# A hybrid decoder layer in f32 on one core: attention values in pairs, other queues at both ends, and another order of output parts

## The chip, the core and the metric

The kernel runs on one of the eight cores of a Trainium2 chip. The metric is device time in microseconds. Kernel and change are each one program with one launch.

## The reference

One step of a one-layer trunk, for a prompt of 2048 tokens and for 8 sequences of 4 new tokens each ("sample", 32 rows). Model width 1024, everything in f32. Cut to what matters:

```
u = rmsnorm(x, g_mix);  z = u @ w_in + b_in            # 1024 -> 1792
q (8 x 64) | k (2 x 64) | v (2 x 64) | xb (512) | yb (512) = split(z)
attn = softmax(q k^T / 8 - slope * distance, window 128, with a sink per head) @ v
xc   = causal conv of width 4 over xb
r, ig = sigmoid(block_diag(xc, w_a)), sigmoid(block_diag(xc, w_i))
a = exp(-8 r softplus(-lam));  h_t = a_t h_{t-1} + sqrt(1 - a_t^2) (ig_t xc_t)
mix = concat(attn, h * gelu(yb))                       # 512 + 512
h1 = x + mix @ w_out + b_out
y  = h1 + (silu(gate) * up) @ w_ffn_out,  gate, up = rmsnorm(h1) @ w_ffn_in    # hidden 2816
y  = rmsnorm(y, g_final)
```

The outputs are y for prompt and sample, and the last keys, values, conv rows and states of both.

## The kernel before, in words

**Tiling.** Activations lie transposed: features on the 128 partitions, tokens along the free dimension. The prompt goes through in four blocks (b = 0 to 3) of 512 tokens. The 32 sample rows ride along with block 0 up to the input projection and with block 3 from the output projection on; there a unit is 544 columns wide and is computed in two halves of 272 (`chunks`, `wide_at`), elsewhere in one piece of 512. A *unit* is a strip of 128 output features: K, V, four Q, eight of the recurrent branch (x and y, `UH` on), eight of the output projection (`U_O`), then those of the FFN. A unit is a sum over 8 tiles of 128 input features (kt). f32 precision comes from three products per tile with operands split in a high and a low part: x_hi w_hi (L724), x_lo w_hi (L725), x_hi w_lo (L726).

**Banks.** PSUM has eight banks: three (`G`, bank0 to bank2) go round for the units, two (`S`, bank3 and bank4) hold scores, two (`TB`) transposes, one (`V`, bank7) the attention values. `bank_of` and `place_of` give a half its bank; `gemm` makes PE wait until the half that used the bank last has been read.

**Order.** Each engine's program is written out by hand and they meet in semaphores. On PE, `mixers` has eight steps s, one per unit of the recurrent branch: `scores(s)` (L859; queries of 128 tokens, four heads), `attend(s - 2)` (L891; probabilities times values), a part of the unit's tiles, in odd steps `gates(s // 2)` (L901), then `probs_T(s - 1)` (L873, transposes of probabilities that POOL has normalised), then the rest of the unit. The scores products take quarters of the array and attend's take half of its columns; the unit products take all of it. ACT and DVE copy the transposed probabilities to SBUF (`pT`, L1313 and L1725); attend waits for these copies. `gates` uses bank7 and a G bank for the first channel group, the S banks for the others.

After step 7 come the *parts* of the output projection: its last four tiles (4 to 7) are the recurrent results, whose last one (`lmix_ready`, DVE L1784) is late, and tiles 0 to 3 the attention (`amix_ready`, L1789). So three units (in the last block three halves) are begun together: first tiles 4 and 5, then 6, then the four attention tiles of each, last tile 7 of each.

**Weights.** SP loads each unit's raw weights into one of two buffers; ACT makes the high part (`split`, L1179) and DVE the low part (L1572) in a ring of three slots. A slot is free when the unit that used it is done. In block 0 the parts of 22 units are also stored to HBM and loaded again in later blocks.

**Start and end.** At the start SP asks for four rows of tiles x_tok, ACT for the identity matrix, the sample rows xs_tok and the vectors. PE transposes x_tok (L1102) and xs_tok (L1126), ACT and DVE sum squares and copy, PE spreads 1/rms along the rows (`along`, L757), and then per tile DVE scales (L1607), ACT makes x_hi (L1228), DVE x_lo (L1613) and PE multiplies for units K and V (`first_units`). At the end four tiles of y_p and one of y_s go out: SP asks in the order y_p 0, 1, 2, y_s in four pieces, y_p 3.

Of the kernel before, what the change touches and what calls it, by code (L numbers as in the profile page):

```python
# [33 lines left out]
P = 128  # L34
# [57 lines left out]
def hymba_layer(nc, x_p, x_s, cache_k, cache_v, conv_in, h_in, units, vecs, w_a, w_i, sinks_p, sinks_s,  # L92
# [3 lines left out]
    DB, DT = x_s.shape[0], x_s.shape[1]  # L96
# [52 lines left out]

    def place_of(b, u, c):  # L150


        j = JOB[b, u, c]
        return j - (j > 3)
# [5 lines left out]
    with ctx:  # L160
# [156 lines left out]
        def bank_of(b, u, c):  # L317
            return S[0] if JOB[b, u, c] == 3 else G[place_of(b, u, c) % 3]
# [211 lines left out]
        def _(sp):  # L530
# [40 lines left out]

            for m in range(QB):
                sp.dma_start(x_tok[:, m, :], x_p[0, m * P:(m + 1) * P, :]).then_inc(row_in[m], 16)
            for u in range(NU):
                load_raw(0, u)
                if RAW <= u < KEEP + RAW:
                    store_parts(u - RAW)
# [7 lines left out]
            for n, m in enumerate(END):  # L585
                sp.wait_ge(end_act, n + 1)
                sp.wait_ge(end_dve, n + 1)
                if m < QB:
                    y_out[m % 2].by(sp.dma_start(y_p[0, bass.ds((NB - 1) * T + m * P, P), :], x_tok[:, m, :]))
                else:  # L590
                    for t in range(DT):
                        sp.dma_start(y_s[:, t, :], y_tok[t * DB:(t + 1) * DB, 0, :]).then_inc(ys_out, 16)
# [3 lines left out]
        def _(pool):  # L596
# [80 lines left out]
            for done_, n in ((cache_out, 2), (kv_out, N_KV_OUT), (state_out, N_STATE_OUT), (ys_out, DT)):  # L677
                pool.wait_ge(done_, 16 * n)
# [5 lines left out]
        def _(pe):  # L684
# [10 lines left out]
            def gemm(b, wide, u, hi, lo, tile_ready=None, kts=None, only=None, begins=0):  # L695
# [11 lines left out]
                for c, (c0, c1) in enumerate(chunks(wide)):  # L707
                    if only is not None and c != only:
                        continue

                    j = JOB[b, u, c]
                    if first and j > 3:
                        pb, pu, pc = JOBS[j - 4 if j < 7 else j - 3]
                        if wide_at(pb, pu) and pc == 0:
                            pe.wait_ge(read_in_half if pu < UO0 else freed_half, pu + 1 if pu < UO0 else pu - UO0 + 1)
                        else:
                            units_read(pe, pb, pu + 1)
                    out = bank_of(b, u, c)[:, 0:c1 - c0]
                    for kt in kts:
                        if tile_ready and (c == 0 or only == c):  # L720
                            tile_ready(kt)
                        h = w_h[:, kt * P:(kt + 1) * P]
                        l = w_l[:, kt * P:(kt + 1) * P]
                        nc.tensor.matmul(out, h, hi[:, kt, c0:c1], start=(first and kt == kts[0]), stop=False)  # L724
                        nc.tensor.matmul(out, h, lo[:, kt, c0:c1], start=False, stop=False)  # L725
                        mm = nc.tensor.matmul(out, l, hi[:, kt, c0:c1], start=False, stop=(kt == kt_of[u] - 1))  # L726
                    if wide and c == 0 and final:
                        mm.then_inc(gemm_half, 1)
# [110 lines left out]
            def mixers(b, last):  # L839
# [65 lines left out]
                for s in range(NUN):  # L905
                    scores(s)
                    if s >= 2:
                        attend(s - 2)
                    wide = wide_at(b, UH + s)
                    if wide:  # L910
                        gemm(b, wide, UH + s, x_hi, x_lo, None, None, 0)
                    else:
                        cut = KT // 2 if s % 2 == 0 else KT - 3 if s == 1 else KT - 2
                        gemm(b, wide, UH + s, x_hi, x_lo, None, list(range(cut)))
# [24 lines left out]
                ahead = [(0, 0), (0, 1), (1, 0)] if last else [(0, 0), (1, 0), (2, 0)]  # L939
# [8 lines left out]
                attend(NUN - 1)  # L948
                for m, c in ahead:
                    part(m, recurrent[2:3], c)  # L950
                for m, c in ahead:
                    part(m, list(range(KT - LC)), c)
                for m, c in ahead:
                    part(m, recurrent[3:], c)
                if last:
                    part(1, None, 1)
# [161 lines left out]

            pe.wait_ge(ident_here, 16)
            for m in range(QB):  # L1120
# [15 lines left out]
            alongx_done.by(along(rstd_x, True))  # L1136
            first_units()
# [14 lines left out]
        def _(act):  # L1152
# [13 lines left out]
            act.dma_start(ident[:, :], ident_in).then_inc(ident_here, 16)  # L1166
            act.dma_start(xs_tok[:, :], x_s.rearrange("b t d -> t b d")).then_inc(xs_in, 16)
# [334 lines left out]
            split(0, 0)  # L1502
# [5 lines left out]
            for kt in FIRST_ACT[:2]:  # L1508
                first_moved(kt)
            x_keep(0, True)  # L1510
            first_moved(FIRST_ACT[2])
# [21 lines left out]
            for n, m in enumerate(END):  # L1533
# [4 lines left out]
                else:  # L1538
                    act.wait_ge(state_out, 16 * N_STATE_OUT)
                    act.wait_ge(smp_pe, 9)  # L1540
                    A(y_tok[0:NS, 0, 0:512], o[0:NS, :], ACT.Copy, scale=rstd_t[0:NS, m:m + 1]).then_inc(end_act, 1)


        @block.vector
        def _(dve):
# [474 lines left out]
            for kt in FIRST_DVE[:2]:  # L2020
                first_moved(kt)
            reciprocals(0, True, std_x, rstd_x, stdx_ready, rstdx_ready)
            first_moved(FIRST_DVE[2])
# [159 lines left out]
```

## Time and profile before

| | us |
|---|---|
| median of 3 runs | 2217.58 |
| lowest, highest | 2216.32, 2218.53 |
| profiled execution | 2216.64 |
| its span in the trace | 2214.5 |
| PE busy in it | 2182.7 (99%) |
| DVE busy | 1155.6 (52%) |
| ACT busy | 835.4 (38%) |
| mean granted clock of PE | 0.997 |

Times in the trace count from the start of the span. An engine's busy time is the time in which at least one of its instructions runs; matmuls overlap, so the pace is read from one start to the next. What stands in brackets behind a row is the idle time just before it and what ended it. The granted clock has two levels, 1.2 and 2.4 GHz; 1.00 is the higher.

### The profile page before, as it was taken

Reading aid. Unit: us, or ns where it says so; the run is one execution under the profiler, and the core shown is the slowest. Engines: PE = TensorE matmul, PEld = TensorE weight load, DVE = VectorE, ACT = ScalarE, POOL = GpSimd, SP = SyncE. Lnnn points to the kernel's source line nnn. Section 1 sums busy time; section 2 is a strip of 40 time slices with the busy share of each in tenths; the row PEclk is TensorE's granted clock in tenths of the full one; section 3 lists DMA queues with packets and bytes.
Section 4 is the critical chain, followed back from the end, with each engine's and each line's share of the span. In section 5 each row is a group of like instructions: output and inputs, shape, how many; then the busy total and the mean of one; then the engine's idle time right before and its main releaser. Section 6 shows DMA issues by size and latency. Waiting matters only on the chain.

```text
span 2214.5 us, 29659 instructions
## 1 busy us (share of the span) xinstructions
PE 2182.7 (99%) x12131; PEld 1839.8 (83%) x12131; DVE 1155.6 (52%) x1981; ACT 835.4 (38%) x1372; POOL 155.6 (7%) x186
## 2 busy tenths in 40 slices
PE   7999999999999999999999999999999999999997
PEld 7878888888877888888877888888887799999997
DVE  5777535445376544434448654444537654444443
ACT  5773323242374322224258322223336532222223
POOL 1330000000041000000013000000003200000000
PEclk9999999999999999999999999999999999999999
DMA  7455224222634222232453432222244332222221
GB/s 272 155 186 187 90 89 153 96 86 86 214 129 171 95 95 95 90 100 83 138 180 113 171 100 94 93 95 96 87 179 153 117 105 87 86 86 86 88 88 66
DMA packets 78923, 264.81 MB, mean 120 GB/s; under 512 B 9521, under 2 KB 13825, under 8 KB 78772
## 3 DMA queue, kind: packets, MB, share of 16 engines
q1 hardware_dynamic: 73504, 246.58, 32.3%
q0 software_dynamic: 3232, 9.80, 1.3%
q10 hardware_dynamic: 2052, 6.53, 0.7%
q8 instruction: 97, 1.59, 0.3%
q14 instruction: 38, 0.31, 0.0%
HBM read 231.04 MB, written 32.84 MB: 119 GB/s over the span
## 4 chain that ended last, share of the span: by engine, by line
PE 92%; DVE 3%; ACT 2%; issue 1%; POOL 1%; DMA 0%; ACTq 0%; DVEq 0%; POOLq 0%
PE bank L724 29%; PE bank L726 29%; PE bank L725 29%; PE bank L891 1%; PE bank L873 1%; POOL s_p L611 1%; PE bank L859 1%; PE bank L901 1%; DVE s_p L1706 1%; PE bank L821 0%; PE bank L773 0%; DMA xs_tok<-in_x_sample 0%; ACT s_p L1306 0%; DVE xc L1742 0%; DVE xc L1737 0%
## 5 line engine op out<-in xcount | busy, mean ns | idle before, releaser
L724 PE MATMUL bank<-x_hi,w_hi 128*128 128x512 f32 (+1 forms) x2224 | 787.2, 354 | 3.3 <-DVE x_lo L1613 3.2
L726 PE MATMUL bank<-x_hi,w_lo 128*128 128x512 f32 (+1 forms) x2224 | 780.3, 351 | 0.0
L725 PE MATMUL bank<-x_lo,w_hi 128*128 128x512 f32 (+1 forms) x2224 | 779.0, 350 | 0.0
L1179 ACT ACTIVATE w_hi<-w_raw 128x1024 fp32r<-128x1024 f32 (+1 forms) x294 | 304.6, 1036 | 1006.1 <-PE bank L726 973.7
L724 PEld LDWEIGHTS bank<-x_hi,w_hi 128*128 128x128 f32 x2224 | 418.9, 188 | 70.6 <-issue 11.0
L725 PEld LDWEIGHTS bank<-x_lo,w_hi 128*128 128x128 f32 x2224 | 419.2, 188 | 56.7 <-issue 1.7
L726 PEld LDWEIGHTS bank<-x_hi,w_lo 128*128 128x128 f32 x2224 | 418.7, 188 | 56.4
L1572 DVE TENSOR_TENSOR w_lo<-w_raw,w_hi 128x1024 fp32r<-128x1024 f32 (+1 forms) x294 | 351.4, 1195 | 123.7 <-ACT w_hi L1179 123.7
L724 PE MATMUL bank<-a_hi,w_hi 128*128 128x512 f32 (+1 forms) x1168 | 412.0, 353 | 2.8 <-DVE a_lo L1784 1.5
L726 PE MATMUL bank<-a_hi,w_lo 128*128 128x512 f32 (+1 forms) x1168 | 411.5, 352 | 0.0
L725 PE MATMUL bank<-a_lo,w_hi 128*128 128x512 f32 (+1 forms) x1168 | 410.9, 352 | 0.0
L724 PEld LDWEIGHTS bank<-a_hi,w_hi 128*128 128x128 f32 x1168 | 219.4, 188 | 38.1 <-issue 5.4
L725 PEld LDWEIGHTS bank<-a_lo,w_hi 128*128 128x128 f32 x1168 | 219.5, 188 | 30.9
L726 PEld LDWEIGHTS bank<-a_hi,w_lo 128*128 128x128 f32 x1168 | 219.3, 188 | 30.7
L611 POOL TENSOR_SCALAR s_p<-s_p,rec 128x256 f32<-128x256 f32 x128 | 127.2, 1009 | 1360.3 <-DVE rec L1720 1360.3
L1999 DVE TENSOR_TENSOR hT<-bank,hT 128x512 f32<-128x512 f32 (+1 forms) x120 | 70.8, 592 | 243.8 <-PE bank L726 243.4
L1586 DVE TENSOR_TENSOR a<-bank,rinv 128x512 f32<-128x512 f32 (+1 forms) x110 | 65.1, 592 | 215.6 <-PE bank L726 213.6
L1586 DVE TENSOR_TENSOR gt<-bank,rinv 128x512 f32<-128x512 f32 (+1 forms) x110 | 64.9, 591 | 203.0 <-PE bank L726 202.5
L1306 ACT ACTIVATE s_p<-s_p,nm 128x256 f32<-128x256 f32 x128 | 63.2, 495 | 32.2 <-DVE sd L1712 31.8
L1466 ACT ACTIVATE a_hi<-a 128x512 fp32r<-128x512 f32 (+1 forms) x88 | 56.3, 639 | 35.8 <-DVE a L1984 33.8
L1980 DVE SCALAR_TENSOR_TENSOR gt<-th,gt 128x512 f32<-128x512 f32 (+1 forms) x88 | 61.1, 694 | 5.0 <-ACT th L1463 5.0
L1984 DVE SCALAR_TENSOR_TENSOR a<-gt,a 128x512 f32<-128x512 f32 (+1 forms) x88 | 61.7, 701 | 3.0
(306 smaller groups left out, 1580.5 us busy)
## 6 DMA issues: line engine op xcount, KB each, us to landing
w_raw<-in_units SPq DMA_DIRECT2D x222, 512.0 KB, 3.2
w_raw<-in_units SPq DMA_DIRECT2D x64, 448.0 KB, 3.1
w_hi<-keep SPq DMA_DIRECT2D x51, 512.0 KB, 3.3
w_lo<-keep SPq DMA_DIRECT2D x51, 512.0 KB, 4.5
w_kept<-keep SPq DMA_DIRECT2D x30, 512.0 KB, 4.4
keep<-w_hi SPq DMA_DIRECT2D x22, 512.0 KB, 5.3
keep<-w_lo SPq DMA_DIRECT2D x22, 512.0 KB, 6.4
x_tok<-in_x_prompt POOLq DMA_DIRECT2D x12, 512.0 KB, 5.3
```

The costliest lines, as they stand in the source:

```text
L611: ins = nc.gpsimd.tensor_scalar(s_p[:, s % 2, hh, :], s_p[:, s % 2, hh, :], rec[:, qb % 2, head:head + 1], None, ALU.mult)
L724: nc.tensor.matmul(out, h, hi[:, kt, c0:c1], start=(first and kt == kts[0]), stop=False)
L725: nc.tensor.matmul(out, h, lo[:, kt, c0:c1], start=False, stop=False)
L726: mm = nc.tensor.matmul(out, l, hi[:, kt, c0:c1], start=False, stop=(kt == kt_of[u] - 1))
L1179: A(w_hi[:, slot(b, u), 0:n], w_raw[:, u % RAW, 0:n], ACT.Copy).then_inc(w_hi_ready, 1)
L1306: A(s_p[:, s % 2, hh, :], s_p[:, s % 2, hh, :], ACT.Exp, bias=nm[:, s % 2, hh:hh + 1], accum_out=rs[:, s % 2, hh:hh + 1])
L1466: act_hi.by(A(a_hi[:, f, 0:w], a32[:, n % 2, 0:w], ACT.Copy))
L1572: TT(w_lo[:, slot(b, u), 0:n], w_raw[:, u % RAW, 0:n], w_hi[:, slot(b, u), 0:n], ALU.subtract).then_inc(w_ready, 1)
L1586: return lambda src, c0, c1: TT(dst(c0, c1), src, rinv[:, c0:c1], ALU.mult)
L1980: link(STT(out=gt[:, 0:w], in0=th[:, 0:w], scalar=1.0, in1=gt[:, 0:w], op0=ALU.add, op1=ALU.mult))
L1984: act_f.by(STT(out=a32[:, n % 2, 0:w], in0=gt[:, 0:w], scalar=0.5, in1=a32[:, n % 2, 0:w], op0=ALU.mult, op1=ALU.mult))
L1999: evacuate(b, last, u, lambda src, c0, c1: TT(hT[:, m, c0:c1], src, hT[:, m, c0:c1], ALU.add))
```

## The change

Six edits.

1. In `mixers`, attend(s - 3) and attend(s - 2) both stand behind scores(s) in the odd steps from 3 on, and none in even steps. In even steps of narrow blocks one more of the unit's tiles (5 of 8) comes ahead of `probs_T`. Since attend(0) also held PE back until gates(0) had been read, step 2 of block 0 now waits for that by itself.
2. In the last block a fourth half, (1, 1), is begun with the other three. Its bank is S[0], and it leaves the turns of the G banks (`TURNS`).
3. In block 0 the parts are in another order: unit 0 ends after the first two attention tiles of unit 2.
4. The identity and xs_tok are asked for on SP's queue, ahead of x_tok and behind its second tile.
5. y_s goes out as one request on ACT's queue, after all copies of the end.
6. PE multiplies the identity by itself, 8 times ahead of the first transposes and 20 times after `along`; nobody reads the results. At the start ACT's first split stands behind its first copy, and copies stand behind `x_keep` (ACT) and behind the reciprocals (DVE).

```diff
+    J_LAST = JOB[NB - 1, U_O[1], 1]
+    TURNS = [j for j in range(len(JOBS)) if j not in (3, J_LAST)]
+    TURN = {j: i for i, j in enumerate(TURNS)}
     def place_of(b, u, c):
-        j = JOB[b, u, c]
-        return j - (j > 3)
+        return TURN[JOB[b, u, c]]
...
-            return S[0] if JOB[b, u, c] == 3 else G[place_of(b, u, c) % 3]
+            return S[0] if JOB[b, u, c] in (3, J_LAST) else G[place_of(b, u, c) % 3]
...
+            sp.dma_start(ident[:, :], ident_in).then_inc(ident_here, 16)
             for m in range(QB):
                 sp.dma_start(x_tok[:, m, :], x_p[0, m * P:(m + 1) * P, :]).then_inc(row_in[m], 16)
+                if m == 1:
+                    sp.dma_start(xs_tok[:, :], x_s.rearrange("b t d -> t b d")).then_inc(xs_in, 16)
...
-                else:
-                    for t in range(DT):
-                        sp.dma_start(y_s[:, t, :], y_tok[t * DB:(t + 1) * DB, 0, :]).then_inc(ys_out, 16)
...
-                    if first and j > 3:
-                        pb, pu, pc = JOBS[j - 4 if j < 7 else j - 3]
+                    if first and j == J_LAST:
+                        sc_read.wait(pe, b, NUN)
+                        gates_read.wait(pe, b, LC)
+                    elif first and j > 3:
+                        pb, pu, pc = JOBS[TURNS[TURN[j] - 3]]
...
                     scores(s)
-                    if s >= 2:
+                    if s >= 3 and s % 2 == 1:
+                        attend(s - 3)
                         attend(s - 2)
+                    if s == 2 and wide:
+                        gates_read.wait(pe, b, 1)
...
-                        cut = KT // 2 if s % 2 == 0 else KT - 3 if s == 1 else KT - 2
+                        cut = KT // 2 + 1 if s % 2 == 0 else KT - 3 if s == 1 else KT - 2
...
-                ahead = [(0, 0), (0, 1), (1, 0)] if last else [(0, 0), (1, 0), (2, 0)]
+                ahead = [(0, 0), (0, 1), (1, 0), (1, 1)] if last else [(0, 0), (1, 0), (2, 0)]
...
                 attend(NUN - 1)
+                for m, c in ahead[3:]:
+                    part(m, recurrent[:2], c)
                 for m, c in ahead:
                     part(m, recurrent[2:3], c)
...
+                if b == 0:
+                    part(0, list(range(KT - LC)))
+                    part(1, list(range(KT - LC)))
+                    part(2, list(range(2)))
+                    part(0, recurrent[3:])
+                    part(2, list(range(2, KT - LC)))
+                    part(1, recurrent[3:])
+                    part(2, recurrent[3:])
...
-                if last:
-                    part(1, None, 1)
...
+            def idle_products(bank, n):
+                for _ in range(n):
+                    nc.tensor.matmul(bank[:, 0:P], ident[:, :], ident[:, :], start=True, stop=True)
+
             pe.wait_ge(ident_here, 16)
+            idle_products(V, 8)
...
             alongx_done.by(along(rstd_x, True))
+            pe.wait_ge(moved_dve, 2)
+            idle_products(G[0], 20)
             first_units()
...
-            act.dma_start(ident[:, :], ident_in).then_inc(ident_here, 16)
-            act.dma_start(xs_tok[:, :], x_s.rearrange("b t d -> t b d")).then_inc(xs_in, 16)
...
-            split(0, 0)
...
-            for kt in FIRST_ACT[:2]:
-                first_moved(kt)
+            first_moved(FIRST_ACT[0])
+            split(0, 0)
             x_keep(0, True)
+            first_moved(FIRST_ACT[1])
...
+            act.wait_ge(end_act, len(END))
+            act.wait_ge(end_dve, len(END))
+            act.dma_start(y_s.rearrange("b t d -> t b d"), y_tok[0:NS, 0, :]).then_inc(ys_out, 16)
```

PE at the start of the program, before:

```order
L1102 MATMUL bank<-ident,x_tok 128x128 x14
L1126 MATMUL bank<-ident,xs_tok 128x32 x8
L1102 MATMUL bank<-ident,x_tok 128x128 x18
L757 MATMUL bank<-ident,rstd_x 128x128 x4
L760 MATMUL bank<-ident,rstd_x 128x32
L724 MATMUL bank<-x_hi,w_hi 128x272
```

and of the change (L1146 is the idle product, L1125 the transposes):

```order
L1146 MATMUL bank<-ident 128x128 x8
L1125 MATMUL bank<-ident,x_tok 128x128 x14
L1156 MATMUL bank<-ident,xs_tok 128x32 x8
L1125 MATMUL bank<-ident,x_tok 128x128 x18
L766 MATMUL bank<-ident,rstd_x 128x128 x4
L769 MATMUL bank<-ident,rstd_x 128x32
L1146 MATMUL bank<-ident 128x128 x20
L733 MATMUL bank<-x_hi,w_hi 128x272
```

Two groups of idle products have come in; the rest keeps its order.

PE in block 1, steps 4 and 5 of the mixer, before (L859 scores, L891 attend, L901 gates, L873 transposed probabilities; "..." stands for unit products):

```order
L859 MATMUL bank<-kT,qT 64x192 x8
L891 MATMUL bank<-pT,v_tok 64x256 x4
...
L873 MATMUL bank<-ident,s_p 128x128 x8
...
L859 MATMUL bank<-kT,qT 64x192 x8
L891 MATMUL bank<-pT,v_tok 64x256 x4
...
L901 MATMUL bank<-xc,gates_w 128x512 x2
L873 MATMUL bank<-ident,s_p 128x128 x8
```

and of the change (L868, L900, L910, L882):

```order
L868 MATMUL bank<-kT,qT 64x192 x8
...
L882 MATMUL bank<-ident,s_p 128x128 x8
...
L868 MATMUL bank<-kT,qT 64x192 x8
L900 MATMUL bank<-pT,v_tok 64x256 x8
...
L910 MATMUL bank<-xc,gates_w 128x512 x2
L882 MATMUL bank<-ident,s_p 128x128 x8
```

The attend of the even step has moved behind that of the odd step, eight instructions in a row.

PE in the last block behind the last attend, before (bank0, bank1, bank2 are the halves (0, 0), (0, 1), (1, 0)):

```order
L891 MATMUL bank7<-pT_102,v_tok_63 64x256 x4
L724 MATMUL bank0<-a_hi_55,w_hi_51 128x272
L725 MATMUL bank0<-a_lo_56,w_hi_51 128x272
L726 MATMUL bank0<-a_hi_55,w_lo_52 128x272
L724 MATMUL bank1<-a_hi_55,w_hi_51 128x272
L725 MATMUL bank1<-a_lo_56,w_hi_51 128x272
```

and of the change (bank3 is the half (1, 1)):

```order
L900 MATMUL bank7<-pT_102,v_tok_63 64x256 x4
L733 MATMUL bank3<-a_hi_55,w_hi_51 128x272
L734 MATMUL bank3<-a_lo_56,w_hi_51 128x272
L735 MATMUL bank3<-a_hi_55,w_lo_52 128x272
L733 MATMUL bank3<-a_hi_55,w_hi_51 128x272
L734 MATMUL bank3<-a_lo_56,w_hi_51 128x272
```

The half that came last as a whole before now runs beside the other three, tile by tile.

## Rows read from the trace of the kernel before

**Rows 1.** Page, part 1: busy us, share of the span, instructions.
```profile
PE 2182.7 (99%) x12131; PEld 1839.8 (83%) x12131; DVE 1155.6 (52%) x1981; ACT 835.4 (38%) x1372; POOL 155.6 (7%) x186
```

**Rows 2.** PE's waits: instruction, released by, us in total, times, longest.
```profile
PE bank L891 <- ACT pT L1313: 2.6, 4, 0.8
...
PE bank L873 <- POOL s_p L611: 0.9, 2, 0.5
PE bank L859 <- ACT ii L1321: 0.6, 2, 0.3
...
PE bank L724 <- DVE a_lo L1789: 0.2, 1, 0.2
```

**Rows 3.** Timeline of the start: start us, us, engine, instruction, idle before.
```profile
2.21 0.39 ACTq L1166 DMA_DIRECT2D ident<-in_ident_in  x1
...
9.44 3.17 PE L1102 MATMUL bank<-ident,x_tok 128*128 128x128 f32 x14 [9.44 <-DMA ident<-in_ident_in]
9.50 1.23 DVE L2011 CUSTOM_DVE_ANT_0 hT<-x_tok 128x1024 f32<-128x1024 f32 x1 [0.36 <-DMA x_tok<-in_x_prompt]
...
11.99 1.06 ACT L1501 ACTIVATE y_tok<-xs_tok 32x1024 f32<-32x1024 f32 x1 [3.85 <-DMA xs_tok<-in_x_sample]
...
13.15 2.18 PE L1102 MATMUL bank<-ident,x_tok 128*128 128x128 f32 x18
...
15.85 1.13 PE L757 MATMUL bank<-ident,rstd_x 128*128 128x128 f32 x8 [0.51 <-ACT xT L1493]
...
20.48 0.60 PE L724 MATMUL bank<-x_hi,w_hi 128*128 128x272 f32 x1 [3.17 <-DVE x_lo L1613]
```

**Rows 4.** Busy by stretch (us, busy): PE, PEld, DVE, ACT, POOL, PEclk, DMA share, GB/s.
```profile
20.00:30.00 10.00, 9.52 (x55) 9.42 (x56) 9.78 (x15) 5.09 (x9) 0.00 (x0) 0.70 0.88 332
...
45.00:60.00 15.00, 14.97 (x120) 14.73 (x118) 2.45 (x2) 4.70 (x8) 0.00 (x0) 1.00 0.91 321
...
98.60:118.60 20.00, 19.68 (x166) 16.65 (x168) 19.14 (x50) 17.98 (x40) 9.01 (x9) 1.00 0.45 159
```

**Rows 5.** Timeline of DVE, the last two x_lo of the start.
```profile
29.74 1.53 DVE L1613 TENSOR_TENSOR x_lo<-a,x_hi 128x544 fp32r<-128x544 f32 x2
```

**Rows 6.** Timeline of PE in block 1, steps 1 and 3.
```profile
612.15 0.88 PE L859 MATMUL bank<-kT,qT 64*64 64x192 f32 x16
...
613.29 0.40 PE L725 MATMUL bank<-x_lo,w_hi 128*128 128x512 f32 x1
...
630.67 0.88 PE L859 MATMUL bank<-kT,qT 64*64 64x192 f32 x16
631.48 1.08 PE L891 MATMUL bank<-pT,v_tok 128*64 128x256 f32 x8
...
632.83 0.39 PE L725 MATMUL bank<-x_lo,w_kept 128*128 128x512 f32 x1
```

**Rows 7.** DVE's waits in block 0, 98.6 to 130 us.
```profile
DVE pT L1725 <- PE bank L873: 0.4, 2, 0.2
```

**Rows 8.** Timeline of POOL and of PE in block 1, step 2.
```profile
621.68 3.63 POOL L611 TENSOR_SCALAR s_p<-s_p,rec 128x256 f32<-128x256 f32 x4 [2.48 <-DVE rec L1720]
...
626.92 1.04 PE L873 MATMUL bank<-ident,s_p 128*128 128x128 f32 x8
```

**Rows 9.** Timeline of ACT and PE, output units of block 0.
```profile
156.70 1.06 ACT L1179 ACTIVATE w_hi<-w_raw 128x1024 fp32r<-128x1024 f32 x1 [4.45 <-PE bank L726]
...
159.08 0.50 PE L724 MATMUL bank<-a_hi,w_hi 128*128 128x512 f32 x1 [1.06 <-DVE w_lo L1572]
```

**Rows 10.** Timeline of PE, output parts of the last block.
```profile
1753.45 0.36 PE L724 MATMUL bank<-a_hi,w_hi 128*128 128x272 f32 x1 [1.55 <-DVE a_lo L1784]
```

**Rows 11.** Timeline of SP at the end.
```profile
2204.39 2.86 SPq L592 DMA_DIRECT2D out_y_s<-y_tok  x4
2207.36 0.37 SPq L589 DMA_DIRECT2D out_y_p<-x_tok  x1
```

**Rows 12.** What the core's DMA moved, 40 slices of 2195 to 2214 us.
```profile
GB/s 0 0 0 0 0 0 0 0 0 0 0 0 0 34 0 0 0 250 397 423 388 405 405 414 414 276 86 181 379 405 267 0 0 0 0 0 0 0 0 0
```

More of the change, by code:

```diff
@@ L676, in _ @@
             pool.dma_start(nh_p[0], outr_p[CONV_W - 1:CONV_W, :]).then_inc(state_out, 16)
-            for done_, n in ((cache_out, 2), (kv_out, N_KV_OUT), (state_out, N_STATE_OUT), (ys_out, DT)):
+            for done_, n in ((cache_out, 2), (kv_out, N_KV_OUT), (state_out, N_STATE_OUT), (ys_out, 1)):
                 pool.wait_ge(done_, 16 * n)
@@ L948, in mixers @@
                 attend(NUN - 1)
+                for m, c in ahead[3:]:
+                    part(m, recurrent[:2], c)
                 for m, c in ahead:
                     part(m, recurrent[2:3], c)
[L951 to L954, printed above, removed]
-                if last:
-                    part(1, None, 1)
+                if b == 0:
[6 more added lines that the diff above has]
+                    part(2, recurrent[3:])
+                else:
+                    for m, c in ahead:
+                        part(m, list(range(KT - LC)), c)
+                    for m, c in ahead:
+                        part(m, recurrent[3:], c)
                 for u in U_O[2 if last else 3:]:
@@ L2019, in _ @@
             first_sum(3)
-            for kt in FIRST_DVE[:2]:
-                first_moved(kt)
+            first_moved(FIRST_DVE[0])
             reciprocals(0, True, std_x, rstd_x, stdx_ready, rstdx_ready)
+            first_moved(FIRST_DVE[1])
             first_moved(FIRST_DVE[2])
```

## The prediction

> **What bounds the kernel now.** I read the page first. TensorE (PE) is busy for 2182.7 of 2214.5 us [rows 1], so the weight products are the floor and only the time in which PE waits, runs at the lower clock or changes mode can be won. The list of PE's waits came second: ahead of its four passes through the mixer it waits 2.6 us for copies of transposed probabilities, and under 1 us each for POOL and for gate values [rows 2]. Third, the timeline of the start: the first weight product stands at 20.48 us [rows 3]. Fourth, the busy table by stretch: the granted clock is 0.70 in 20 to 30 us, and 1.00 later at 120 products in 15 us, 0.125 us each [rows 4]. Then the stretches in which the change acts: a mixer [rows 6], the output parts [rows 9, 10] and the stores at the end [rows 11, 12].
>
> The sum is made against the profiled execution, 2216.64 us (its span 2214.5 us), which lies 0.94 us under the median of 2217.58.
>
> **Start.** The identity is asked for at 2.21 us on ACT's queue, behind nothing of its own, but on the chip's transfers beside 2 MB of x_tok, and PE starts with it at 9.44; xs_tok holds ACT until 11.99, and split, copies, square root and PE's four row products at 15.85 follow in series [rows 3]. Now SP asks for the identity first and for xs_tok between rows 1 and 2. The last row of x_tok lands at 9.50 today [rows 3]; 192 KB now stand ahead of it on its queue, at 332 GB/s [rows 4] 0.6 us at most, since part of them crossed its way before too; I take 10.0. From there: DVE's square sum 1.2 us, two square roots and one copy on ACT 1.1, so PE's row products begin near 12.35 instead of 15.85: 3.5 us. Behind them ACT has one more copy ahead of x_hi, DVE its split; I charge 0.1 us. The first product could start at 17.1.
>
> The idle products are new. Four such f32 products of 128 columns with their loads fill 8 records in 1.13 us at the higher clock [rows 3], 0.26 us each; 20 of them take 5.1 us, from 13.7 to 18.9. They end 1.8 us after the first x_lo is there, so they delay the first product, but at 18.9 PE comes straight from work and should be at the higher clock. Today it comes from 3.2 us of waiting and runs its first products at about half pace; the last of the 96 products of the first two units starts near 34.7. With 96 x 0.126 = 12.1 us from 18.9 it ends near 31.0. DVE does not stop this: its last two x_lo end at 31.27 today [rows 5], 27.9 after a shift of 3.4, plus two tiles of products (3.0) is 30.9. That gives about 3.9 us. Bounds: 5 (clock and rows better) and 0 (next paragraph). The first 8 idle products lie in time in which PE waits for rows 0 and 1, and row 3 is what counts; cost nothing, and if row 3 came 2 us sooner they would still be hidden.
>
> What the clock does decides. The first 14 transposes took 3.17 us, 0.23 each, and the 18 at 13.15 took 2.18, 0.12 each [rows 3]: the clock rose while PE did little but transposes. I go by that. The Trainium skill (TensorE: Matmul & The Clock Gate, Part 4: PE-mode transpose) says transposes do not count as activity that brings the full clock; the two rows speak against it. By it the row products and idle products would run at the lower level, and that is the first rival.
>
> A second rule speaks against moving requests between queues: the Trainium skill (DMA: Bandwidth & Descriptors, Issuing engines are not separate DMA queues) says that it saves only issue time, because all queues interleave on the same engines. By it the identity would have come early already. The trace shows 64 KB asked for at 2.21 and not used before 9.44 [rows 3], so here the queue matters. If the rule held, transposes would still run from 9.44 to 15.33 and the row products begin 0.5 us earlier than now, not 3.5.
>
> **Values in pairs.** In each of four blocks three pairs of attends stand behind one scores instead of behind two. Scores alone, to the second product behind them, take 613.29 - 612.15 = 1.14 us; scores and attend 632.83 - 630.67 = 2.16 [rows 6]. So an attend costs 1.02 us. Its 8 records take 1.08 with the last one 0.38 long, so they follow each other by 0.10: 0.80 of pure work [rows 6]. A second attend directly behind the first should cost 0.80: 0.2 us a pair, 0.6 us a block. Bounds 0 and 0.22. Besides, attend(0) moves from step 2 to step 3, and its wait for the copy (2.6 us over four blocks, 0.6 to 0.8 each) [rows 2] goes. Blocks 1 to 3: 3 x (0.6 + 0.6) = 3.6 us.
>
> What is late next? In even steps probs_T comes sooner. In block 1 POOL ends at 621.68 + 3.63 = 625.31 and PE transposes at 626.92 [rows 8]; without wait and attend (0.61 + 1.02) and with the one tile more ahead of it (3 x 0.23) it comes at 625.98: 0.67 us to spare. The copies that attend(s-3) reads are a step older than before. Scores of odd steps start earlier by 1 us, far behind the softmax that frees their banks.
>
> Block 0 is another matter. Its steps work on 544 columns and DVE also splits weights: in 98.6 to 118.6 DVE is busy 19.14 of 20 us [rows 4]. There PE's waits for gate values (0.6) and probabilities [rows 2] come from DVE's chain, and a faster PE only waits longer. DVE itself waits 0.4 us for PE's transposes in this stretch and its successor [rows 7] and some 0.3 in the one ahead, and those come earlier now. I take 0.7 us for block 0; bounds 0 and 2.3.
>
> **Order of block 0's parts.** Unit 3 of the output waits 1.06 us for w_lo [rows 9], whose ring slot is freed by the end of unit 0: ACT's split at 156.70, first product at 159.08, 2.6 us from the end of unit 0 near 156.5. Today two parts of three products (6 x 0.231 = 1.4 us) lie between; afterwards two tiles of attention and two last parts, 12 x 0.231 = 2.77. The wait goes: 1.1 us, plus a switch of 0.1 once; I take 1.2, bounds 0.9 and 1.2. The last recurrent tile, now wanted earlier, was ready 1.4 us before that place.
>
> **Fourth half sum.** In the last block PE waits 1.55 us for the last a_lo [rows 10], 0.2 for the attention one [rows 2], and 0.4 of the 0.9 us for probabilities [rows 2]. The half (1, 1) in the scores' bank puts 7 tiles x 3 x 0.126 = 2.6 us of existing work ahead of that wait. Both a_lo waits go: 1.7. The 0.4 goes if DVE's chain gets ahead by the shorter step 6, as it should (DVE waited there for PE's unit). 2.1 us, bounds 1.5 and 2.1. No product is added.
>
> **End.** SP asks four times for y_s, 2204.39 to 2207.25, and only then for the last y_p, 2207.36 [rows 11]; its data was ready at 2204.98. ACT now asks once for y_s. The issue comes 2.3 us sooner, but 2.2 MB must drain: from 2203.1 at some 410 GB/s it ends near 2208.5 instead of 2209.7 [rows 12]. I take 1.2 us, bounds 0.9 and 2.3.
>
> **Sum.** 3.9 + 3.6 + 0.7 + 1.2 + 2.1 + 1.2 = 12.7 us; 2216.64 - 12.7 = 2203.9, on the scale of the median 2204.9.
>
> **Rivals.** (a) The start brings nothing, because the requests land no sooner (part of this chance) or the clock is low: the 20 idle products take twice 5.1, end near 23 to 24 or rise midway; the start brings 0 and the sum 8.8: 2208.8. For it: a break of a microsecond ahead of them. Against: the 18 transposes at 0.12. (b) Switching between attends costs as before and block 0 gives nothing: 2.4 + 0.7 less, with the copies' wait still gone: 2208.0. For it: nobody has put two attends side by side in this trace. (c) What PE wins is waited for later at the weights: everything won ahead of the last block (3.9 + 0.7 + 1.2 + 2.4) is lost: 2213.1. Against: each unit's loads are released by PE's own progress, and DMA is 36% busy. (d) Slower: the even steps. With attend gone from ahead of probs_T only the 0.67 us remain; if POOL's 3.6 to 4.8 us norm comes later than that by t in each of 12 even steps, PE pays 12 t, and above t = 1.06 us all is lost; at t = 1.5 it is 2223. For it: POOL's row ends that near. Against: DVE, which releases POOL, is itself ahead when PE's even unit ends sooner. That a term simply isn't there is (a) to (c).
>
> **Numbers.** Forecast 0.63, (a) 0.14, (b) 0.11, (c) 0.08, (d) 0.04. 0.2% of the median is 4.4 us, about what can be told from no change: 2213.1. Forecast, (a), (b) fall under it, (c) lies on it: faster 0.88, same 0.08, slower 0.04. The range reaches from the upper bounds (2204.9 less 4: 1.1 at the start, 1.6 in block 0, 1.1 at the end) to beyond (a): 2200.5 to 2209.5.
>
> **What would show it.** First weight product at 18 to 19.5 us and granted clock near 1.00 in 20 to 30; PE's waits for pT, for w_lo at output unit 3 and for the last a_lo gone; two attends in 1.9 us; span from the last matmul to the end shorter by 1.2. Wrong if the first product is behind 20 us, or if waits for s_p or gates above 1 us stand in even steps of blocks 1 to 3.

## The result, and the profile after

The changed kernel takes 2205.05 us (median of 5 runs, 2204.99 to 2205.6), the kernel before 2217.58 (5 runs, 2216.32 to 2218.53): a ratio of 0.9945 with a 95% interval of 0.9933 to 0.9956, 12.5 us less. The forecast was 2204.9. The profiled execution took 2204.99 us, its span is 2203.1. Two executions at a low mean granted clock (0.632 in one of the kernel before, 0.85 in one of e10) took 3185.77 and 2370.93 us and are in no ratio below.

The page of after, part 1 (answers to [rows 1]): PE's busy time is 2.4 us longer, though the span is 11.4 shorter.

```profile
PE 2185.1 (99%) x12187; PEld 1845.8 (84%) x12187; DVE 1153.5 (52%) x1981; ACT 835.0 (38%) x1372; POOL 156.6 (7%) x186
```

All waits of PE in after (us in total, times, longest) answer to [rows 2]. The waits for pT, w_lo and a_lo are gone; of 0.9 us for s_p 0.4 is left, in block 0.

```profile
PE bank L1146 <- DMA ident<-in_ident_in: 2.6, 1, 2.6
PE bank L766 <- ACT xT L1523: 0.9, 1, 0.9
PE bank L868 <- ACT ii L1351: 0.7, 2, 0.5
PE bank L1125 <- DMA x_tok<-in_x_prompt: 0.6, 2, 0.4
PE bank L745 <- ACT sq L1276: 0.6, 1, 0.6
PE bank L882 <- POOL s_p L617: 0.4, 1, 0.4
PE bank L868 <- issue: 0.3, 1, 0.3
PE bank L733 <- ACT ii L1351: 0.2, 1, 0.2
```

The start of after, on the timeline (start us, us, engine, instruction, idle before), answers to [rows 3]:

```profile
0.73 0.39 SPq L578 DMA_DIRECT2D ident<-in_ident_in  x1
...
2.62 3.78 PE L1146 MATMUL bank<-ident 128*128 128x128 f32 x16 [2.62 <-DMA ident<-in_ident_in]
...
6.20 2.34 PE L1125 MATMUL bank<-ident,x_tok 128*128 128x128 f32 x14
...
10.94 1.23 DVE L2045 CUSTOM_DVE_ANT_0 hT<-x_tok 128x1024 f32<-128x1024 f32 x1
...
13.26 1.13 PE L766 MATMUL bank<-ident,rstd_x 128*128 128x128 f32 x8 [0.89 <-ACT xT L1523]
...
14.65 4.73 PE L1146 MATMUL bank<-ident 128*128 128x128 f32 x40
...
17.11 0.72 DVE L1647 TENSOR_TENSOR x_lo<-th,x_hi 128x544 fp32r<-128x544 f32 x1
...
19.14 0.37 PE L733 MATMUL bank<-x_hi,w_hi 128*128 128x272 f32 x1
```

To find where the rest of the time went I took the same instructions in both traces and compared their start times. These are the ones of after:

```profile
56.66 0.88 PE L868 MATMUL bank<-kT,qT 64*64 64x192 f32 x16 [0.28 <-issue]
...
139.62 1.08 PE L900 MATMUL bank<-pT,v_tok 128*64 128x256 f32 x8
...
599.64 0.88 PE L868 MATMUL bank<-kT,qT 64*64 64x192 f32 x16
...
677.34 1.08 PE L900 MATMUL bank<-pT,v_tok 128*64 128x256 f32 x8
...
1734.87 1.08 PE L900 MATMUL bank<-pT,v_tok 128*64 128x256 f32 x8
...
2187.55 1.05 PE L745 MATMUL bank<-ones,sq 128*128 128x1 f32 x8 [0.56 <-ACT sq L1276]
2190.71 1.04 PE L801 MATMUL bank<-ident,yg 128*128 128x128 f32 x8
```

| from ... to | before, us | after, us | gained | forecast |
|---|---|---|---|---|
| start of the span ... scores(0) of block 0 | 60.25 | 56.66 | 3.59 | 3.9 |
| ... last attend of block 0 | 83.99 | 82.96 | 1.03 | 0.7 |
| ... scores(0) of block 1 | 461.33 | 460.02 | 1.31 | 1.2 |
| mixers of blocks 1, 2 (each) | 78.82, 78.81 | 77.70, 77.70 | 1.12, 1.11 | 1.2, 1.2 |
| mixer of block 3 | 77.76 | 76.16 | 1.60 | 1.2 + 0.4 |
| last attend of block 3 ... row sums of y | 455.11 | 452.68 | 2.43 | 1.7 |
| row sums ... last transposes | 3.16 | 3.16 | 0 | 0 |
| last transposes ... end of the span | 11.67 | 12.39 | -0.72 | +1.2 |

The stretches between the blocks' mixers and the next scores differ by 0.04 us at most: what is won stays won. The sum is the span's 11.4 us. The execution profiled before lay 0.94 us under its median, the one after 0.06 under, so the medians differ by about 1 us more than the profiles.

### The profile page after: what moved, and what is told of

Its sections match the earlier page's. It is cut to its first block, busy times and chain, and to the rows that moved or that the text cites. A ratio compares the mean times of both kernels' runs of the same rounds, so it can differ in the third digit from the quotient of the medians.

```text
span 2203.1 us, 29774 instructions
## 1 busy us (share of the span) xinstructions
PE 2185.1 (99%) x12187; PEld 1845.8 (84%) x12187; DVE 1153.5 (52%) x1981; ACT 835.0 (38%) x1372; POOL 156.6 (7%) x186
## 3 DMA queue, kind: packets, MB, share of 16 engines
q8 instruction: 97, 1.59, 0.3%
## 4 chain that ended last, share of the span: by engine, by line
PE 95%; DVE 2%; ACT 1%; issue 1%; POOL 0%; DMA 0%; SPq 0%; DVEq 0%; ACTq 0%; POOLq 0%
PE bank L733 30%; PE bank L735 30%; PE bank L734 30%; PE bank L900 1%; PE bank L882 1%; PE bank L910 1%; PE bank L868 1%; PE bank L830 0%; PE bank L782 0%; POOL s_p L617 0%; DMA x_tok<-in_x_prompt 0%; DVE s_p L1740 0%; ACT s_p L1336 0%; PE bank L1146 0%; DVE xc L1776 0%
```

## The experiments

The start varies from run to run. In the four profiles with the old requests (before, e4, e6, e7) DVE's sum of row 3 began at 9.50, 9.41, 10.64 and 10.43 us, but the scores of block 0 came at 60.25, 61.25, 60.03 and 61.20: there it is not the rows that set the start. PE's last 18 transposes took 2.18, 4.10, 2.55 and 3.89 us, and the two in which they kept half pace are the two late ones. In after, e1, e2 and e11 the scores (56.66, 57.30, 57.42, 57.18) follow row 3 by 45.7 to 45.8 us each time. The two means lie 3.5 us apart, so the 3.59 of the table is a fair value. So the verdicts rest on stretches between two instructions of one profile, and the medians only confirm them.

### The parts of the mixers and the last block, alone (e4, e6, e7)

Each is one edit made on the kernel before. Pairs:

```diff
-                    if s >= 2:
+                    if s >= 3 and s % 2 == 1:
+                        attend(s - 3)
                         attend(s - 2)
-                        cut = KT // 2 if s % 2 == 0 else ...
+                        cut = KT // 2 + 1 if s % 2 == 0 else ...
```

> The kernel before with the values in pairs alone (attend(s-3) and attend(s-2) behind scores(s) of odd steps; one more tile ahead of the probabilities' transposes in even steps). Theory 1 (the mixers' gain of 1.0 to 1.2 a block comes from the pairs alone): 4.3 to 4.8 us faster than before, 2212.8 to 2213.3, the waits for pT gone. Theory 2 (part of what the mixers gained was handed on by the earlier start or by the order of block 0's parts): blocks 1 to 3 still gain 1.1 each, block 0 less than 0.5: 3.3 to 3.8 us faster, 2213.8 to 2214.3.

Measured 2212.77 us (10 runs), ratio 0.9977 (0.9968 to 0.9987) to a before of 2218.14. Mixers: block 0 82.99 instead of 83.99, block 1 77.71, block 2 77.69, block 3 76.17: 1.00, 1.11, 1.12 and 1.59 us, the same as in after to 0.03 us. 4.8 us come from the pairs alone. The last block stayed at 455.11.

The order of block 0's parts (the diff is that of the change, the branch for b == 0):

> The kernel before with only the new order of block 0's output parts. Theory 1 (the gain of 1.3 us is the wait of unit 3 for w_lo and one switch, whatever else is changed): from the last attend of block 0 to the first scores of block 1 it takes 460.0 us instead of 461.33, the wait for w_lo is gone; the time falls by 1.3 us. Theory 2 (the wait only moves: to the next unit's w_lo, or back as soon as PE reaches the part at the old time): 461.1 to 461.4 us, no gain.

460.01 us instead of 461.33, and the wait for w_lo is no longer in the list: 1.32 us. Median 2215.92 (11 runs) against 2217.88, ratio 0.9992 (0.9983 to 1.0001), in which one such term is hardly seen. Theory 1.

The fourth half sum, with TURNS and the bank of the scores as in the change:

> The kernel before with only the fourth half sum in a bank of the scores in the last block (and the tables of turns that it needs). From the last attend of the last block to the first row sums of y it takes 455.11 us in before and 452.68 in after, 2.43 less, where I had 1.7. Theory 1 (the two waits for a_lo and what PE loses when it restarts behind them and in the half's own start, all in this edit): 2.3 to 2.5 less, and block 3's mixer stays at 77.76: the time 2.3 us under before. Theory 2 (0.7 of it comes from the pairs, which leave PE later relative to DVE): 1.6 to 1.8 less.

452.68 us instead of 455.11, 2.43 less, and the mixer of block 3 as before, 77.77; median 2215.51 (11 runs), ratio 0.9992 (0.9983 to 1.0001). Theory 1. The 0.7 us above the two waits can be read in before's timeline: between two products of 0.126 us stand three breaks. The first product behind the last a_lo starts 1.83 us behind the one ahead, though the wait is 1.55 [rows 10], and the next follows by 0.20 and not 0.126. The break at the attention a_lo takes 0.46 + 0.20, its wait 0.17; the separate start of (1, 1) behind the wait 0.28 + 0.20. Less the usual pace that is 1.77 + 0.40 + 0.22 = 2.4 us. So these waits cost their own length and some 0.22 us for the restart.

### The end (e1, e2)

```diff
-            act.dma_start(y_s.rearrange("b t d -> t b d"), y_tok[0:NS, 0, :])   # ACT
+                else:                                                           # SP, ahead of the last y_p
+                    for t in range(DT):
+                        sp.dma_start(y_s[:, t, :], y_tok[t * DB:(t + 1) * DB, 0, :]).then_inc(ys_out, 16)
```

> The kernel after, with the sample outputs y_s stored as before: four requests of 8 rows on SP, ahead of the last y_p. Theory 1 (the tail is the one request of ACT, whose last 1.3 us run at about 100 GB/s after everything else has drained): the four requests hold the last y_p back to about 2195.3, but end at full rate, so the stores end near 2197.0 to 2197.6 instead of 2198.2: the time falls by 0.6 to 1.2 us, to 2203.9 to 2204.5. Theory 2 (my forecast's: the four issues of 2.9 us ahead of the last y_p are what the end waits for): the time rises by 1.2 us, to 2206.2.

e2 has the one request in that place on SP.

> The kernel after, with y_s stored in one request (the same one, 32 rows) by SP ahead of the last y_p, not by ACT behind everything. Theory 1 (late start of the one request at about 100 GB/s): it starts 0.7 us sooner, beside the y_p stores, and the last y_p is asked for at about 2193.6, before the first three have drained: the stores end near 2197, the time is 1.0 to 1.6 us under after, 2203.5 to 2204.1. Theory 2 (the request's own shape sets the end wherever it stands): no more than 0.3 us from after.

Last transposes to the end of the span: e1 11.72 us, e2 12.40, after 12.39, before 11.67. Medians 2204.84 and 2205.39; e1's 0.21 us under after is less than theory 1 said, since in its profiled execution the rows came 0.7 us later at the start (scores at 57.30). Theory 1 is right for e1 in the stretch and wrong for e2: moving the request gains nothing, its form keeps the tail. What the core's DMA moved in 40 slices of 2187 to 2204 us (0.425 us each), in after:

```profile
GB/s 0 0 0 0 0 0 0 0 0 116 414 386 405 414 395 405 395 414 395 405 366 366 106 87 116 58 0 0 0 0 0 0 0 0 0 0 0 0 0 0
```

and in e1:

```profile
GB/s 0 0 0 0 0 0 0 0 0 0 0 279 405 395 434 395 386 395 434 405 241 96 145 386 386 405 58 0 0 0 0 0 0 0 0 0 0 0 0 0
```

In after the 128 KB of y_s move at about 100 GB/s as a tail of four slices, and in e2, where they are asked for ahead of the last y_p, they are again the tail (125, 87, 116, 77, 19). In e1 (and before, [rows 12]) there is a hole of three slices ahead of the last y_p instead. By these times SP's issues set its length: the last y_p is asked for at 2195.89 in e1 and begins to move some 0.8 us later, as the first does behind its request at 2190.99. At what rate y_s could move in that hole can't be told from it. The change filled the hole and grew the tail. On ACT's queue 36 packets are counted in after for the 32 rows; the four requests take 64 (640 less 576), the four y_p requests 576 for 512 rows. So beyond the rows it is 16 packets for a request of y_p, 8 for one of 8 rows and 4 for the single one, which has 4 outer groups. That fits a request on 4 of the 16 engines at a quarter of the 400 GB/s, but no view here shows the engines one by one.

### The idle products (e3, e11)

```diff
-            idle_products(G[0], 20)
```

> The kernel after without the 20 idle products ahead of the first weight product (the first 8 stay). Theory 1 (they buy the full clock): the first weight product is at 17.8 us instead of 19.1, but the granted clock in 20 to 30 us falls back to about 0.7, and PE is 1 to 3 us behind at the scores of block 0: time 2206 to 2208. Theory 2 (the clock is up anyway from the transposes, row products and the shorter break of 3 us): the first units are bound by DVE's copies; the scores come 0 to 1.2 us sooner, time 2203.9 to 2205.

Median 2205.69, ratio 0.9945 (0.9933 to 0.9958) to 2218.14. The first weight product moves to 17.52 us, but from DVE's sum of row 3 to the scores it takes 46.28 us (10.53 to 56.81) instead of 45.72. So the 20 are worth 0.56 us, less than theory 1 said (1 to 3), and the gain of theory 2 isn't there. Busy by stretch, PE alone (us, busy, PEclk, DMA share, GB/s), in e3:

```profile
14.00:16.00 2.00, 0.31 (x2) 0.72 0.50 141
16.00:18.00 2.00, 0.48 (x2) 0.50 0.90 209
18.00:20.00 2.00, 2.00 (x10) 0.50 1.00 248
20.00:22.00 2.00, 2.00 (x12) 0.57 1.02 399
```

and in after:

```profile
14.00:16.00 2.00, 2.00 (x18) 1.00 0.42 107
16.00:18.00 2.00, 2.00 (x21) 1.00 0.73 191
18.00:20.00 2.00, 2.00 (x20) 1.00 0.92 250
```

In e3 the granted clock goes to 0.50, the 1.2 GHz level, while PE waits 3.2 us for x_lo; in after, with products in that wait, it stays at 1.00. The first 8 idle products, taken out by themselves:

> The kernel after without the first 8 idle products (the 20 stay). Theory 1 (my prediction's: they lie in time in which PE waits for the rows, and change nothing): from DVE's second square sum (row 3) to the scores of block 0 it takes 45.7 us as in after, the time stays within 0.3 us of 2205.05. Theory 2 (PE's first transposes run at half pace, 0.22 us each, as behind any break, and the 8 products keep that away from the rows): PE is later at row 3 by 1 us or more, and the time from row 3 to the scores grows by 0.3 to 1 us.

From row 3 to the scores 45.76 us (11.42 to 57.18), median 2205.43: theory 1, they change nothing. Without them PE's 14 transposes take 3.22 us and the 18 at 10.17 take 3.85; with them 2.34 and, in parts of 7 and 11, 0.98 and 1.42. The idle products show the two paces on one and the same instruction: the first 8 take 0.45 us each in after (2.62 to 6.20), the 20 take 0.22 (14.65 to 19.14). Half pace at the beginning is real, but with the new requests those transposes are not what the start waits for.

### The requests and the order of ACT's work (e5, e9, e12)

e5 is the kernel before with the identity first and xs_tok between rows 1 and 2, both on SP.

> The kernel before with only the requests moved: the identity first on SP's queue, the sample rows between rows 1 and 2 of x_tok on SP's, none of both on ACT's. No idle products, ACT's and DVE's order at the start as before. Theory 1 (the place in the queue sets the start): identity used at about 2.6 us instead of 9.44; the first weight product at 17.5 to 18.5 instead of 20.48, at a low clock behind its 3 us wait; the scores of block 0 at 57.3 to 58 instead of 60.25, the time 2.3 to 3 us under before, about 2215. Theory 2 (my rival a, the rule that all queues interleave on the same engines): the identity lands no earlier than row 1 or 2 of x_tok, the gain is at most 0.5 us.

Median 2215.53 (11 runs), ratio 0.999 (0.9981 to 0.9998). The identity is there before row 0 (PE starts with row 0, at 5.70), so theory 2 is out. The medians differ by 2.35 us, as theory 1 has it, but not by its path: the first weight product is at 19.35 (17.5 to 18.5 expected), and the scores come at 59.47, only 0.8 us ahead of before. The profiled before is one of the two early ones; against the other two it is 1.7 us. The timeline of ACT in e5 shows what took the place of the wait:

```profile
12.20 1.06 ACT L1180 ACTIVATE w_hi<-w_raw 128x1024 fp32r<-128x1024 f32 x1 [2.41 <-issue]
13.16 0.37 ACT L1505 ACTIVATE xT<-bank 128x256 f32<-128x256 f32 x1
```

The split of unit 0 stands ahead of the copy of the samples; its w_raw is requested behind all rows, and ACT, in order, holds the copy from 9.8 to 13.16. In before the same split stood behind xs_tok of 11.99 [rows 3], which hid it.

> The kernel after with ACT's and DVE's order of the start as before: the split of unit 0 ahead of the copy of the samples' transposes, two copies ahead of the reciprocals and of x_along. Requests and idle products stay. Theory 1 (the queue's gain is only to be had with this order: ACT's split waits for w_raw, which lands near 12.2, and all that follows on ACT with it): the first weight product moves from 19.1 to about 20 us or more, and it takes 46.5 to 47.3 us from DVE's sum of row 3 to the scores instead of 45.7: 0.8 to 1.6 us slower, about 2206.2. Theory 2 (my prediction's: one copy and the split count 0.1 us): within 0.3 us of after.

2207.9 us, ratio 0.9957 (0.9941 to 0.9973) to 2217.14: from row 3 to the scores it takes 48.16 us (11.61 to 59.77), 2.45 more than in after, beyond what theory 1 gave. ACT waits 2.39 us for w_raw there, the row products begin at 15.15, 3.54 us behind row 3 instead of 2.32, and behind PE's break of 1.66 us ahead of its last four transposes the clock falls (0.50 in 16 to 18 us):

```profile
14.00:16.00 2.00, 1.50 (x11) 0.99 0.15 37
16.00:18.00 2.00, 2.00 (x10) 0.50 0.70 131
18.00:20.00 2.00, 2.00 (x14) 0.66 0.78 264
```

So of the 2.45 us 1.2 are the chain up to the row products, and 1.1 the idle products, which take 5.61 us at the lower clock instead of 4.49.

> The kernel before with the identity and the sample rows asked for on SP's queue behind rows 0 and 1 of x_tok, so at 2.1 us, the time at which ACT asks for the identity in before (2.2 us, used at 8.5 to 9.4 in four runs). Theory 1 (a queue is worked off in its order, and requests of another queue come behind what is already under way): the identity is there just behind row 1, PE starts between 6.5 and 7.3 us. Theory 2 (the rule that it doesn't matter on which queue a request stands; only that it is asked for earlier helped): PE starts at 8.4 us or later, as in before.

PE starts at 6.04 with the identity, sooner than theory 1 said and 2.4 to 3.4 us ahead of what ACT's queue gave, though it is asked for behind 1 MB, at 1.65 us (I had expected 2.1). This is one run; 0.56 us of the difference is the earlier request, and theory 2 is out. That the queue as such matters is not shown, though: in before all four rows are asked for between 0.73 and 2.55 us, so at 2.21 the fourth is being asked for, while in e9 two rows stand ahead of the identity. Serving by the order of asking, over both queues, would give both times, and one row of e9 fits it (out, queue, KB, us from asking to landing):

```profile
vec<-in_vecs ACTq DMA_DIRECT2D x1, 37.0 KB, 4.8
```

ACT asks for the vectors at 2.44 and they are there at 7.2, ahead of the samples, which SP asked for at 2.12 and which are used at 8.09. An identity asked for first, but on ACT's queue, was not tried. The Trainium skill (DMA: Bandwidth & Descriptors, Issuing engines are not separate DMA queues) has it that moving a request between queues saves only issue time; these runs neither bear it out nor refute it, since every move here changed the order of asking too.

e9's scores come at 57.74, 47.27 us behind row 3, against 48.58 in e5 and 48.16 in e12, though ACT waits 2.54 us for w_raw there as well: the clock fell later (granted clock 0.80 in 18 to 20 us, 0.50 in e5). So with ACT's old order the start depends on when the clock falls, by 1.3 us between these two runs.

### Versions that are better (e8, e10)

```diff
-   sp.dma_start(xs_tok[:, :], x_s.rearrange("b t d -> t b d"))
+   sp.dma_start(xs_tok[:, :], x_s.rearrange("b t d -> (b t) d"))
-   A(xT[:, :, T:W], V[:, 0:KT * NS].rearrange("p (k n) -> p k n", k=KT), ACT.Copy)
+   A(xT[:, :, T:W].rearrange("p k (t b) -> p k t b", b=DB),
+     V[:, 0:KT * NS].rearrange("p (k b t) -> p k t b", k=KT, b=DB), ACT.Copy)
-   idle_products(G[0], 20)
+   idle_products(G[0], 14)
```

(and the identity's columns in the samples' row product put in the same order). e8 stores y_s with two requests on ACT and two on SP; e10 reads and stores the samples between rows 1 and 2: END = (0, 1, QB, 2, 3), four requests on SP.

> The kernel after with three edits that act in different places. (i) The sample rows are read as 32 flat rows (a token's order b t, put right in ACT's copy and in the row product of the samples), not as 4 groups of 8. (ii) 14 idle products ahead of the first weight product, not 20. (iii) y_s in four requests of 8 rows, two on ACT, two on SP behind the last y_p. Theory 1 (a request goes out over as many of the 16 engines as its outermost count, so 4 groups run at 100 GB/s and 8 rows at more): (i) the samples land with row 2, at least 0.5 us ahead of row 3, and PE's wait for them is under 0.5 us; (iii) the last store ends 1.2 to 1.8 us closer to the last product, so that from the last transposes' start to the span's end it takes 10.6 to 11.2 us instead of 12.39. (ii): the first product comes at x_lo, 17.8 us with full clock, but DVE's second x_lo (20.6) is next, so 0.2 us at the scores. In all 2203.0 to 2203.8. Theory 2 (the end is bound by the drain of 2.2 MB or by fixed costs, not by the request's shape): 12.2 us or more at the end, 2204.5 to 2205.

2203.79 us, ratio 0.9938 (0.9925 to 0.995) to 2217.88. (i) ACT begins the samples' squares at 8.34 without a wait, where it waited 0.50 to 1.38 us in the eight profiles with the grouped request on SP; row 3's sum begins at 10.08, in e10 at 10.10, against 10.47 to 11.71 in those eight. SP issues the flat load in 0.43 us instead of 0.82 and asks for rows 2 and 3 that much sooner; how much of the gain is this, and how much the load's own rate, is not told apart. (ii) The first weight product is at 17.04 at granted clock 1.00, but PE then waits 0.51 us for w_lo and 0.26 for x_lo: row 3 to the scores is 45.72, as with 20. DVE is the bound there. (iii) 12.17 us at the end: theory 2.

> The kernel e8 (flat sample rows, 14 idle products) with the samples' outputs read, and stored by SP in four requests of 8 rows, between rows 1 and 2 of y_p. Theory 1 (what is left behind the drain of 2.2 MB at 400 GB/s is the small requests at the tail): the stores' last slices at 100 to 200 GB/s go, the last store ends 0.4 to 0.8 us closer to the last product, 11.4 to 11.8 us from the last transposes' start to the span's end instead of 12.17: 2203.0 to 2203.4. Theory 2 (the four small requests break the stream wherever they stand): 12.2 us or more, 2203.8 or more.

2203.46 us, ratio 0.9937 (0.9923 to 0.9951) to 2217.14, the best: 1.6 under after. The end takes 11.71 us, but theory 1 fails on its reason: the hole is back in the slices, now earlier, and ends some 0.8 us after SP asks for the next y_p (2193.13).

```profile
GB/s 0 0 0 0 0 0 0 77 395 414 405 395 414 366 87 145 241 405 434 386 414 405 260 0 0 0 0 0 0 0 0 0 0 0 0 0 0 0 0 0
```

With before's end the stretch measured 11.66 to 12.19 us in seven profiles, with one request 12.32 to 12.42 in five, so 11.71 is a good end of the old kind and no better, and the 0.72 us that the end lost against the profiled before is near the upper end of what these two ranges allow (0.1 to 0.8). What the start gives (about 0.9) is shown by the anchors: scores at 55.80 and 55.81.

## Why the prediction was right, and where it was not

**Start, 3.9 forecast, 3.59 measured.** From row 3 on the working held: row products 2.32 us behind it (2.35 in mine), x_lo at +6.9 (+7.1), 96 products at 0.126 us behind 19.14. Row 3 was 0.94 us later than the 10.0 that I took; I charged 0.6 us for 192 KB at the full rate; the flat form of the samples' load brings row 3 to 10.1 (e8, e10), so the grouped form is at least part of what I priced too low. The idle products ended before 19.4, and I was right that DVE stands just behind (e8), so their delay of the first product cost next to nothing. But my reading of the clock is not borne out. I took 0.23 and 0.12 us per transpose [rows 3] for a rise of the clock. The stretches of before (us, PE busy, PEclk, DMA share, GB/s) show the granted clock at 1.00 in both:

```profile
10.00:12.00 2.00, 2.00 (x11) 1.00 0.83 256
12.00:14.00 2.00, 2.00 (x20) 1.00 0.08 31
...
18.00:20.00 2.00, 0.00 (x0) 0.81 0.93 223
20.00:22.00 2.00, 1.52 (x6) 0.50 0.81 221
```

The pace did double there, and so did that of the idle products, at a granted clock of 1.00 both times; whether that is the clock stays open. What is shown is that the 20 idle products keep the granted clock from falling in the wait for x_lo, worth 0.56 us. That the Trainium skill (TensorE: Matmul & The Clock Gate, Part 4: PE-mode transpose) doesn't count transposes as activity is neither borne out nor refuted by these rows: the granted clock stood at 1.00 before the first of them, and fell in a break. Nor is "here the queue matters", my answer to the second rule: the order of asking changed with the queue (e9). And "DVE's and ACT's order 0.1 us" was the costliest miss in the working: without it 2.45 us of the start's gain is not there (e12, 1.1 of it by the clock). The sum came out because I had put the copy ahead of the split in my chain without pricing what happens otherwise.

**Pairs, 3.6 + 0.4 forecast for blocks 1 to 3, 3.83 measured.** Two attends in after:

```profile
623.02 0.88 PE L868 MATMUL bank<-kT,qT 64*64 64x192 f32 x16
623.84 1.95 PE L900 MATMUL bank<-pT,v_tok 128*64 128x256 f32 x16
```

1.95 us against 1.08 for one [rows 6]: the second costs 0.87 where I had 0.80 and the old place 1.02. So a pair saves 0.15 us of switching, not 0.2, and three of them 0.45 a block. The other 0.68 is the wait for the copy, which before had in step 2:

```profile
621.52 0.88 PE L859 MATMUL bank<-kT,qT 64*64 64x192 f32 x16
623.01 1.08 PE L891 MATMUL bank<-pT,v_tok 128*64 128x256 f32 x8 [0.61 <-ACT pT L1313]
624.02 0.50 PE L724 MATMUL bank<-x_hi,w_hi 128*128 128x512 f32 x1
624.36 0.39 PE L725 MATMUL bank<-x_lo,w_hi 128*128 128x512 f32 x1
```

From the scores to the second product it is 2.84 us, against 2.16 without a wait: 0.61 and a restart of only 0.07. No wait in an even step of blocks 1 to 3: rival (d) is out. Rival (b) too.

**Block 0's mixer, 0.7 and 1.03.** I held DVE for the bound and took the lower part of the range; e4 gives 1.00 with nothing else changed.

**Order of the parts, 1.2 and 1.31.** Right, e6.

**Fourth half sum, 1.7 and 2.43.** The mechanism is right, the size is short by the restarts, 0.22 us at each of three breaks.

**End, +1.2 and -0.72: the step that failed.** I read the hole of [rows 12] as SP's four issues, and that holds: it is gone in after. What failed is the next step, "2.2 MB must drain at some 410 GB/s". That is right for the y_p rows alone; the 128 KB of y_s, in one request, move at about 100 GB/s when all else has drained, and so they are a tail. The span from the last transposes to the end, which I had wanted 1.2 us shorter, is 0.72 longer, a miss of 1.9 us. Block 0 and the last block gave 1.2 more than forecast, start and pairs 0.5 less; the profiled times differ by 11.65 us, not 12.7 (2204.99 against 2203.9 by my sum). The medians differ by 12.5 because the profile of before lay 0.94 us under its median and that of after only 0.06. The hit to 0.15 us is partly luck.

**Rivals (a) and (c).** The start brought 3.6 us, and nothing was waited for later: between the blocks the two traces keep their distance to 0.04 us.

Left open: why the first transposes and idle products run at half pace with a granted clock of 1.00; whether ACT's queue is slower than SP's, or only the order of asking counts; how the small requests are dealt out to the DMA engines (that the flat form of the load is quicker is shown, the reason is not; a flat form of the store wasn't tried); and whether the end can go under 11.7 us.

## What to carry to other kernels

Compare two traces at the same instructions, stretch by stretch: on an engine that is 99% busy every stall removed stays removed, and each costs its wait plus a restart (0.07 to 0.23 us here). When a transfer that one queue waits for is brought forward, look at what stands next in that engine's program, since an early wait for something else can take its place (here 2.4 us). Small requests at the end of a kernel cost more than their bytes: four of them held the last big one back, and one, of few outer groups, drained at a quarter of the rate. Moving them changed hole to tail.

## What the runs showed that I had not expected

- Between weight products of 272 columns a break of PE costs about 0.22 us more than the wait in the list: 0.15 to 0.16 ahead of the first product, 0.07 ahead of the second, and as much between two sums without any wait. Ahead of an attend, behind scores, it costs 0.07.
- The identity, asked for at 1.65 us on SP's queue behind 1 MB of rows, is used at 6.04; asked for at 2.21 on ACT's queue, behind three rows or more, at 8.5 to 9.4 (four profiles).
- SP needs 0.82 us to issue the samples' load in groups of 8 rows and 0.43 for the flat one; stores of 8 rows take it 0.71 each (e1), 0.53 in e10 and 1.3 in e8, where they stand behind the last y_p.
- The granted clock is 1.00 in stretches in which transposes pass at half the pace that they reach later. Pace and granted clock have to be read apart.
